# Reordering VectorE's queue in the two feed-forward loops of a two-block transformer kernel

## The reference, cut to what matters

```python
# end of the first block (w_ff1: 1024 x 4096, w_ff2: 4096 x 1024)
h = rms_norm(x, g_mlp[l])
x = x + jnp.square(jax.nn.relu(h @ w_ff1[l])) @ w_ff2[l]
...
# end of the second block (gate, up: 1024 x 2816, down: 2816 x 1024)
hn = rms_norm_2(h, ffn_norm_g[l])
h = h + (jax.nn.silu(hn @ w_ffn_gate[l]) * (hn @ w_ffn_up[l])) @ w_ffn_down[l]
```

## Time and profile before

| | |
|---|---|
| median of 3 runs | 1550.54 us (1550.22 to 1554.56) |
| the profiled execution | 1550.54 us |
| its span, first to last instruction | 1548.7 us |
| PE busy | 1506.8 us, 97% of the span |
| DVE busy | 1006.7 us, 65% |
| ACT busy | 668.4 us, 43% |
| mean granted TensorE clock | 0.991 |
| tile loops of the first feed-forward | 473 to 503, 543.5 to 588.8, 629 to 672.6, 713 to 756.5 us |

### The profile page before, as it was taken

One profiled execution on the slowest core, in us unless ns is written; L12 is line 12 of the kernel. 1 busy time (PEld: TensorE's weight loads), 2 busy tenths in 40 slices (PEclk: granted clock), 3 DMA queues, 4 the chain that ended last, 5 costly groups with the idle time before them and its releaser, 6 DMA issues.

```text
span 1548.7 us, 21935 instructions
## 1 busy us (share of the span) xinstructions
PE 1506.8 (97%) x8122; PEld 1240.2 (80%) x8122; DVE 1006.7 (65%) x1914; ACT 668.4 (43%) x1180; POOL 351.1 (23%) x367
## 2 busy tenths in 40 slices
PE   7999989999999999999999999999999999999997
PEld 5787556788887989898988778866688889889887
DVE  4656676344457959596866787577375677568454
ACT  5533577322245434343456433566444333333232
POOL 3300455100020000000057534445431210120112
PEclk9999999999999999999999999999999999999999
DMA  5662200432222223232221762312422323322221
GB/s 197 135 157 94 70 15 1 136 102 102 82 97 105 91 89 106 100 109 96 96 90 69 171 176 90 116 49 74 144 93 85 109 82 110 109 91 101 96 95 55
DMA packets 47849, 154.28 MB, mean 100 GB/s; under 512 B 5842, under 2 KB 8082, under 8 KB 47744
## 3 DMA queue, kind: packets, MB, share of 16 engines
q1 hardware_dynamic: 43008, 137.63, 25.8%
q0 software_dynamic: 4736, 15.25, 4.5%
HBM read 142.78 MB, written 9.55 MB: 98 GB/s over the span
## 4 chain that ended last, share of the span: by engine, by line
PE 88%; DVE 5%; ACT 3%; DMA 2%; issue 2%; POOL 0%; SPq 0%; DVEq 0%; ACTq 0%
PE PSA L698 71%; PE PSA L909 5%; PE PSA L908 5%; PE PSA L907 5%; PE PSA L977 1%; DMA WR<-w_in 1%; PE PSA L1121 1%; ACT AR L1562 1%; DVE AR L2178 0%; DMA XT<-xT_in 0%; DVE WL L1984 0%; DVE AHL L2271 0%; ACT AHL L1611 0%; DVE Al L1984 0%; ACT WH L1480 0%
## 5 line engine op out<-in xcount | busy, mean ns | idle before, releaser
L698 PE MATMUL PSA<-Ah,WH 128*128 128x512 f32 x1072 | 423.8, 395 | 12.5 <-DVE Al L1992 9.1
L698 PE MATMUL PSA<-Ah,WL 128*128 128x512 f32 x1072 | 419.9, 392 | 0.0
L698 PE MATMUL PSA<-Al,WH 128*128 128x512 f32 x1072 | 419.6, 391 | 0.0
L1984 DVE TENSOR_TENSOR WL<-WR,WH 128x1024 fp32r<-128x1024 f32 (+2 forms) x191 | 240.3, 1258 | 87.2 <-ACT WH L1480 87.0
L1480 ACT CAST WH<-WR 128x1024 fp32r<-128x1024 f32 (+3 forms) x218 | 225.1, 1034 | 122.1 <-PE PSA L698 56.9
L698 PEld LDWEIGHTS PSA<-Ah,WH 128*128 128x128 f32 x1072 | 202.8, 189 | 61.8 <-issue 18.0
L698 PEld LDWEIGHTS PSA<-Ah,WL 128*128 128x128 f32 x1072 | 202.5, 189 | 42.9
L698 PEld LDWEIGHTS PSA<-Al,WH 128*128 128x128 f32 x1072 | 202.8, 189 | 41.7 <-issue 0.7
L2820 POOL TENSOR_TENSOR AR<-AR 128x512 f32<-128x512 f32 (+1 forms) x44 | 55.5, 1271 | 571.2 <-ACT AR L1498 570.3
L2980 POOL TENSOR_TENSOR AR<-AR 128x512 f32<-128x512 f32 x22 | 47.4, 2153 | 267.4 <-DVE AR L2735 267.4
L907 PE MATMUL PSA<-ARR,WH 128*128 128x256 f32 x352 | 99.6, 283 | 0.0
(11 more groups left out here) (415 smaller groups left out, 2838.8 us busy)
## 6 DMA issues: line engine op xcount, KB each, us to landing
WR<-w_in SPq DMA_DIRECT2D x228, 512.0 KB, 3.2
gt_tmp<-AR SPq DMA_DIRECT2D x16, 256.0 KB, 2.2
WR<-w_in SPq DMA_DIRECT2D x8, 384.0 KB, 2.9
XT<-scr_tmp POOLq DMA_DIRECT2D x8, 264.0 KB, 13.6
XT<-scr_tmp POOLq DMA_DIRECT2D x8, 256.0 KB, 14.0
XT<-xT_in POOLq DMA_DIRECT2D x1, 2048.0 KB, 9.1
x_tmp<-XT POOLq DMA_DIRECT2D x1, 2048.0 KB, 7.7
AHL<-gt_tmp SPq DMA_DIRECT2D x8, 256.0 KB, 3.7
```

The costliest lines, as they stand in the source:

```text
L698: return pe.matmul(o, l, r, start=start, stop=stop)
L1984: dv.tensor_tensor(wl, x, wh.bitcast(F), ALU.subtract).then_inc(w_lo, 1)
```

## The change

In the first feed-forward's tile loop, DVE's work on tile n+2's halves, sums_low and weight_sum are placed ahead of the wait for PE's tile n. The weight sum s4 of sub-step 0 is moved out of the products into the tile loop (i = 7). The work on the meta rows is moved from n = 9, 10, 12 to n = 7, 8, 10 on DVE, ACT and PE. In the second feed-forward, s1 moves from i = 6 to i = 7, in front of L2745 and next to s2; s4 moves from the products to i = 7, behind the halves and ahead of the wait for `fu`; pair_sums goes ahead of L2762.

```diff
@@ tensor_program
-                    if n == 10:
+                    if n == 8:
                         pe.wait_ge(n_ma.sem, n_ma.at("squares"))
@@ scalar_program
-                    if n == 9:
+                    if n == 7:
                         ac.wait_ge(d_meta, 16)
                         ac.activation(MSQ, x3[:, :, T:TM], ACT.Square).then_inc(n_ma.sem, 1)
@@ vector_program, products
                     if s == 0 and k == 0:
                         sums_low(ph, g, 3)
-                    if s == 0 and k == 1:
-                        weight_sum(u, "s4")
@@ vector_program, first feed-forward
                     s = 2 * (n % 4)
+                    if n > 1:
+                        split_to(tid["f1", n] + 2)
+                    if i in (2, 4, 6):
+                        sums_low(1, q, i // 2 - 1)
+                    if i > 3:
+                        weight_sum(sub_of(1, q, 0), SUMS[i - 4])
                     result(tid["f1", n])
                     if n > 3:
                         dv.wait_ge(f_hi, n - 3)
                     dv.scalar_tensor_tensor(out=RT[s], in0=bank(2 + n % 4), scalar=0.0, in1=RB["m1"], op0=ALU.max,
                                             op1=ALU.mult).then_inc(f_re, 1)
-                    if n > 1:
-                        split_to(tid["f1", n] + 2)
                     dv.wait_ge(f_hi, n + 1)
                     ...
                     if i % 2:
                         pair_sums(1, q, i // 2, RT[2 * ((n - 1) % 4) + 1], RT[s + 1])
-                    if i in (2, 4, 6):
-                        sums_low(1, q, i // 2 - 1)
-                    if 3 < i < 7:
-                        weight_sum(sub_of(1, q, 0), SUMS[i - 4])
-                    if n == 9:
+                    if n == 7:
                     ...
-                    if n == 10:
+                    if n == 8:
                     ...
-                    if n == 12:
+                    if n == 10:
@@ vector_program, second feed-forward
                         if i in (2, 4, 6):
                             sums_low(2, ci, i // 2 - 1)
+                        if i == 7:
+                            weight_sum(sub_of(2, ci, 0), "s1")
+                            weight_sum(sub_of(2, ci, 0), "s2")
                     dv.wait_ge(u_th, m + 1)
                     dv.wait_ge(u_zr, m + 1)
                     ...
                     if ci < 2 and i > 5:
-                        weight_sum(sub_of(2, ci, 0), "s3" if i == 6 else "s2")
+                        weight_sum(sub_of(2, ci, 0), "s3" if i == 6 else "s4")
                     ...
+                    if ci < 2 and i % 2:
+                        dv.wait_ge(u_t3, m + 1)
+                        pair_sums(2, ci, i // 2, RT[2 * ((m - 1) % 4) + 1], RT[2 * s + 1])
                     dv.wait_ge(f_hi, F_N + m + 1)
                     ...
-                    if ci < 2 and i % 2:
-                        pair_sums(2, ci, i // 2, RT[2 * ((m - 1) % 4) + 1], RT[2 * s + 1])
-                    if ci < 2 and i == 6:
-                        weight_sum(sub_of(2, ci, 0), "s1")
```

## The result

The changed kernel takes 1576.65 us (median of 5 runs, 1573.6 to 1579.06); the kernel before takes 1553.56 (5 runs, 1550.22 to 1558.09). The ratio is 1.015, 95% interval 1.0124 to 1.0176: slower by 23 us. The forecast was 1573, range 1561 to 1580. The profiled execution of the changed kernel took 1578.5 us, with a span of 1576.7, 28.0 more than before.

A forecast was written before the change was run, and what follows sets the result against it. PE, busy 97% of the span, was taken as the bound, with DVE's chain near its need. Quarter 0 8.2, quarters 1 and 2 5.6, quarter 3 3.2, second feed-forward 2.4 and clock 3.4 on 1550.5 gave 1573 us, range 1561 to 1580.

The forecast's parts named there:

- PE never waits in the loops before: Changed loops: PE shows only two waits for DVE, 0.90 and 0.79 us, so at most 1.7 us can be won.
- The 0.6 us at 481.18: Quarter 0, first feed-forward: tile 4's low half ends 0.6 us earlier and takes that off PE's wait there.
- The hole between relu and Bl: First feed-forward's tile loop: DVE's wait for ACT's squares stays empty; the next WL starts 2.63 us after an even relu.
- Two tiles cost 12.38 us with sums: Tile loop's second half: DVE needs 12.38 us per two tiles with weight sums, against PE's 10.88.
- relu 7 is 3.0 us late: Quarters 1 and 2: tile 7's relu and s1's weights come 3.0 us late; PE stops 2.8 each, 5.6 together.
- The slack: Start of product s1: DVE's chain to s1's low half has only 0.2 us to spare before PE needs it.
- Quarter 3 3.2: Quarter 3, even tiles at full width: the cast comes 0.22 us later at i = 4 and 6, together 3.2 us.
- quarter 0 8.2: Quarter 0: relu 7 is 6.83 us late, plus 1.6 for the moved meta rows, less 0.2 slack: 8.2 us.
- The products give nothing back: Products: losing s4's sum frees 1.14 us of DVE each, but PE waits for nothing there, so no gain.
- Second feed-forward 1.2 per chunk: Second feed-forward, i = 7: s1's sum meets POOL's operation; WL 1.44 us late, 1.2 for PE, 2.4 for two chunks.
- The clock: two falls of 1.7 us, 3.4: PE's new stops: two falls to half clock out of six places, 3.4 us; bounds 0 to 10 us.
- The high bound of six: PE's stops: the clock falls at each of six places, 10 us, giving 1580; as a rival, chance 0.15.

The follow-up runs named there:

- the order alone: Kernel before, first feed-forward's halves, sums_low and three old weight sums put ahead of the wait for tile n, nothing else: 1566.36 us against 1551.21, ratio 1.0094.
- alone and together: Alone: kernel before with only the change's second feed-forward part, one time 1553.13 us; together: the changed kernel, 1576.65 us.
- the run with POOL held: Kernel before with the change's second feed-forward part, POOL's operation of tiles 7 and 15 waiting for sum s2: 1560.83 us, one execution.
- the repeated one: The changed kernel run once more, unaltered, beside the version with filled stops: 1576.8 us, ratio to before 1.0166.
- one line undone: Changed kernel with tile n+2's halves behind the relu again, all sums still ahead of it: 1575.68 us, ratio 1.0147.

## Why the prediction was right

- *PE never waits in the loops before, so there is 1.7 us to win and no bound on the loss.* Right. The 0.6 us at 481.18 came back (0.31 of idle is left in the changed kernel's trace, at 482.91), and 777.53's wait stayed at 0.78.
- *The hole between relu and Bl stays empty, and the next WL starts 2.63 us behind an even relu.* Right: 601.62 - 599.00 = 2.62, and with the order alone, 1.9 us of lateness at relu 7 were forecast from it and a11 to s1 came out at 7.35 (7.4). The order, halves and sums together, is more than half of the loss; filling the hole makes the fourth sum free once no transfer is ahead of the relu. That the hole and not the sums ahead of the relu is the larger share of it follows from the rows' sum; no run separates the two.
- *Two tiles cost 12.38 us with sums; relu 7 is 3.0 us late; PE pays 2.8.* Right in sign and place; measured 2.72. The slack is 0.24 to 0.28 us, not 0.2.
- *Quarter 3 3.2, quarter 0 8.2, of which 1.6 for the meta rows.* Measured 3.15, 8.12 and 1.6.
- *The products give nothing back for the sum that they lose.* Right: with the fourth sum moved alone, the time from s1 to s1 is not shorter (20.25 and 20.26), and PE pays all of what exceeds the slack.
- *Second feed-forward 1.2 per chunk, of which 1.1 is the exclusion with POOL.* Measured 1.10, alone and together. That nearly all of it is the exclusion is the sum 2.32 - 1.22 from rows; no run has the chunk without both the overlap and the wait for POOL. By the Trainium skill, SBUF — State Buffer, "Who interferes with whom", the two instructions exclude each other; the run with POOL held agrees, 1.22 and 1.29 apart against 2.32 and 2.21 together.
- *The clock: two falls of 1.7 us, 3.4.* The mechanism was there and the term mis-sized. Its parts were off and its sum was near: three falls with 1.4 each, and 0.17 at each of the three from s1's and s2's late starts, which the forecast put at nothing: 4.7 in that execution; one fall in these three intervals in the repeated one. The high bound of six, which the prediction called the likelier by its citation alone, did not come: no stop of the second feed-forward was followed by a fall. What I took as half of 3.41 us is less, since a matmul of 256 columns takes 213 ns at the low clock and 120 at the high one (starts in the trace), which makes 3.41 x (1 - 120/213) = 1.5.
- *The total.* 22.8 us forecast and 23.1 measured between medians is nearer than the parts allow: the chain came out 0.5 under, the term for the clock 1.3 over in the profiled execution, 4.2 us there lie in stages that the change does not touch, and the number of falls changes from one execution to the next. The agreement to 0.3 us is luck; that of the chain's intervals is not.
- *Not foreseen:* the releaser of the stop at s1. I had named L1984; the trace says "issue", and only DVE's timeline gives it. And the experiment with one line undone showed a wait for a transfer that my way of counting, DVE and ACT alone, leaves out. It was no part of the forecast's sum, because in the changed kernel the halves come early enough (the sum at i = 5 starts right behind them).

Left open: why the second matmul of s1 and s2 comes 0.07 us late when the first had to wait, and what decides whether a stop is followed by a fall.

## What to carry to other kernels

On an in-order engine, work placed ahead of a wait is free only up to the idle time of that wait; here 1.0 us at one tile, and up to three operations of 1.14 each, 3.4 us, were put there. Before moving an operation out of a place, look at what it covered: a low half between relu and Bl hid the other engine's 1.2 us, and nothing took its place. And count the cycle over the whole period against the bound engine's (12.38 against 10.88 here), not by the engine's busy share, which was 63% in that stretch and said nothing.

## What the runs showed of the hardware

Stops of PE of 1.6 to 3.3 us in a stream of dense matmuls were followed, and the longest overlapped, by 3.41 us, or 6.83, at a granted 0.50 (the lower of the two levels, 1.2 GHz), in some executions and not in others (three, two and four of four quarters); with the same stops filled by unused matmuls there was none in the first feed-forward of the one profiled execution. The cost per fall was 1.4 us of a path on which PE is the bound. The delays of the chain repeated to 0.1 us from trace to trace, while the time of the whole kernel moved by some 10 us between executions, so for a question of 1 us the interval between two named instructions was the measurement, and the total was not.
